# Cached keys of the paged cache fetched by one indirect transfer of GpSimd per granule, in a one-core decoder step

## The reference, cut to what matters

```python
def fox_sample(q, k_new, v_new, logf_new, pool_k, pool_v, pool_logf, page_table):
    ...
    k_all = jnp.concatenate([pool_k[page_table].reshape(b, past, h, e).astype(k_new.dtype), k_new], axis=1)
    v_all = jnp.concatenate([pool_v[page_table].reshape(b, past, h, e).astype(v_new.dtype), v_new], axis=1)
    ...
    sc = jnp.einsum('bthe,bshe->bhts', q, k_all).astype(jnp.float32) * scale + cq - ck
    ...
    p = jax.nn.softmax(sc, axis=-1)
    return jnp.einsum('bhts,bshe->bthe', p.astype(v_all.dtype), v_all).reshape(b, t, h * e)
```

## Time and profile before

| | us |
|---|---|
| median of 3 runs | 1396.51 |
| lowest, highest | 1396.45, 1398.31 |
| the profiled execution | 1398.2 |
| its span | 1396.5 |
| TensorE busy | 1320.3 (95%) |
| VectorE busy | 962.0 (69%) |
| ScalarE busy | 551.3 (39%) |
| GpSimd busy | 250.4 (18%) |
| mean granted TensorE clock | 0.976 of full speed |

### The profile page before, as it was taken

How to read it: one execution, slowest core, us unless ns; L and a number is a source line. 1 busy time by engine, 2 the same in 40 slices (tenths; PEclk the granted TensorE clock), 3 DMA queues, 4 the chain that set the end, 5 groups by cost and what they waited for, 6 DMA issues and landing times.

```text
span 1396.5 us, 24365 instructions
## 1 busy us (share of the span) xinstructions
PE 1320.3 (95%) x9293; PEld 1210.4 (87%) x9293; DVE 962.0 (69%) x1391; ACT 551.3 (39%) x908; POOL 250.4 (18%) x242
## 2 busy tenths in 40 slices
PE   6899999988986899999999999999999999999999
PEld 4668788766665767899899999999999999999999
DVE  6757789979886786758868787787888796111111
ACT  6422211145645665534544434434434454010100
POOL 5540013342331242010101101101111100000000
PEclk9799999989998999999999999999999999999999
DMA  8148766669996966432222222221222275332222
GB/s 290 57 136 255 222 189 194 195 186 250 281 268 213 332 211 193 145 102 91 77 67 86 91 76 63 90 90 55 84 92 69 69 275 188 94 93 74 86 73 73
DMA packets 153422, 201.57 MB, mean 144 GB/s; under 512 B 22005, under 2 KB 116237, under 8 KB 152897
## 3 DMA queue, kind: packets, MB, share of 16 engines
q1 hardware_dynamic: 134492, 140.12, 33.1%
q0 software_dynamic: 12848, 46.73, 11.0%
q10 hardware_dynamic: 5964, 13.16, 3.2%
HBM read 169.64 MB, written 29.82 MB: 143 GB/s over the span
## 4 chain that ended last, share of the span: by engine, by line
PE 59%; DVE 13%; SPq 8%; issue 7%; DMA 6%; POOL 3%; ACT 2%; ACTq 1%; DVEq 0%; POOLq 0%
PE ps L1274 8%; PE ps L1275 8%; PE ps L1276 8%; PE ps L1335 5%; PE ps L1336 5%; PE ps L1337 5%; SPq L411 3%; PE ps L1014 2%; SPq L410 2%; PE ps L1015 2%; PE ps L1115 2%; PE ps L1016 2%; DMA upr<-in_w_upL 2%; DMA ring<-in_cache_a_k 2%; PE ps L1138 1%
## 5 line engine op out<-in xcount | busy, mean ns | idle before, releaser
L1274 PE MATMUL ps<-hhi,uph 128*128 128x258 f32 x704 | 201.0, 285 | 4.3 <-issue 1.4
L1275 PE MATMUL ps<-hlo,uph 128*128 128x258 f32 x704 | 199.6, 284 | 0.0
L1276 PE MATMUL ps<-hhi,upl 128*128 128x258 f32 x704 | 199.3, 283 | 0.0
L1014 PE MATMUL ps<-whi,hhi 128*128 128x512 f32 (+1 forms) x376 | 146.6, 390 | 13.7 <-DVE wlo L1857 9.3
L2578 DVE TENSOR_TENSOR dnl<-dnr,dnh 128x896 fp32r<-128x896 f32 (+2 forms) x24 | 27.3, 1136 | 173.1 <-ACT dnh L1770 173.1
L1016 PE MATMUL ps<-whi,hlo 128*128 128x512 f32 (+1 forms) x376 | 143.2, 381 | 0.0
L1015 PE MATMUL ps<-wlo,hhi 128*128 128x512 f32 (+1 forms) x376 | 143.1, 381 | 0.0
L1274 PEld LDWEIGHTS ps<-hhi,uph 128*128 128x128 f32 x704 | 134.0, 190 | 6.0 <-DVE ug L2536 2.1
L1275 PEld LDWEIGHTS ps<-hlo,uph 128*128 128x128 f32 x704 | 134.2, 191 | 0.0
L1276 PEld LDWEIGHTS ps<-hhi,upl 128*128 128x128 f32 x704 | 133.9, 190 | 0.0
L2763 POOL TENSOR_TENSOR upr<-upr 128x512 f32<-128x512 f32 x22 | 29.5, 1340 | 450.4 <-DMA upr<-in_w_upL 373.8
(11 more groups left out here) (338 smaller groups left out, 3597.5 us busy)
## 6 DMA issues: line engine op xcount, KB each, us to landing
upr<-in_w_upL SPq DMA_DIRECT2D x88, 256.0 KB, 3.4
ring<-in_cache_a_k SPq DMA_DIRECT2D x168, 128.0 KB
scr_act<-va SPq DMA_DIRECT2D x22, 516.0 KB, 2.6
ring<-in_cache_a_k ACTq DMA_DIRECT2D x88, 128.0 KB
wst<-in_w_in SPq DMA_DIRECT2D x32, 256.0 KB, 4.2
fr<-scr_act SPq DMA_DIRECT2D x14, 516.0 KB, 5.5
dnr<-in_w_down SPq DMA_DIRECT2D x12, 448.0 KB, 4.4
dnr<-in_w_down SPq DMA_DIRECT2D x10, 512.0 KB, 3.8
```

Of the source, the lines that this page charges most:

```text
L1014: pe.matmul(out, lh, whi[:, sl, 0:w], start=(kc == 0), stop=False)
L1274: pe.matmul(out, hi_, r_hi[:, cs], start=(first and i == 0), stop=False, skip_group_check=not first)
L1275: pe.matmul(out, hi_, r_lo[:, cs], start=False, stop=False, skip_group_check=not first)
L1276: m = pe.matmul(out, lo_, r_hi[:, cs], start=False, stop=(i == 3), skip_group_check=not first)
```

## The change

All 64 key granules are fetched by GpSimd, each with one indirect transfer, as the values are. `load_pages` and its uses go from SP and ACT. On SP `k_load` stays for the window and memory caches alone. The new `k_page` waits for `k_used` (from granule 4 on) and issues the transfer. In the loop over the projection units it stands behind the unit's `inverse_rms`; the granules and their units are those of `K_ASK`, which is unchanged. The first four granules are requested in (0, 4) in place of (0, 5). In the loop over the value loads, `K_BEFORE` gives the key granules that are requested ahead of value load k. The wait for the row table moves to the first four granules. The window and memory caches get semaphores of their own (`cmk_ld`), and a key granule's transfer now counts 16 in place of 64.

```diff
-        kpool = t["cache_a_k"].rearrange("o n p h e -> (o n) p (h e)")
+        krows = t["cache_a_k"].rearrange("o n (p r) h e -> (o n p) (r h e)", r=4)
...
-        def load_pages(sp, pool, seq, group, slot, pages=range(4), dst=ring, sem="ring_ld"):
-
-            for j in pages:
-                page = sp.value_load(ptab[0:1, bass.ds(seq * PAGES + (group * 4 + j), 1)], min_val=0, max_val=NPOOL - 1)
-                sp.dma_start(dst[32 * j:32 * j + 32, slot, :, :].rearrange("p r c -> p (r c)"),
-                             pool[bass.ds(page, 1)].rearrange("o (p r) c -> p (o r c)", r=4))\
-                    .then_inc(S(f"{sem}{slot}"), 16)
+        def page_gather(pool, rows_, n, dst, sem):
+
+            pool.indirect_dma_start(out=dst.rearrange("p r c -> p (r c)"), out_offset=None, in_=rows_,
+                                    in_offset=bass.IndirectOffsetOnAxis(ap=gtab[:, 0, n:n + 1], axis=0)).then_inc(sem, 16)
...
+        K_BEFORE = {2: [NKP + 2], 4: [NKP + 3]}
+        for g_ in sorted(K_STEP):
+            if K_STEP[g_] + 4 < NKA:
+                K_BEFORE.setdefault(next(k_ for k_ in range(4, NV) if v_step[k_ - 4] >= g_ + 2), []).append(K_STEP[g_] + 4)
...
             def k_load(n):
 
                 sp.wait_ge(S("k_used"), n - 3)
-                if n < NKA:
-                    load_pages(sp, kpool, n // 8, n % 8, n % 4)
-                else:
-                    cm_load(sp, ring[:, n % 4], n - NKA, S(f"ring_ld{n % 4}"), "k")
+                cm_load(sp, ring[:, n % 4], n - NKA, S(f"cmk_ld{n % 4}"), "k")
...
-                if k == (0, 5):
-                    sp.wait_ge(S("const_ld"), 96)
-                    sp.wait_ge(S("x_split"), 3 * KC)
-                    sp.wait_ge(S("x_sq"), 3 * KC)
-                    for s4 in range(4):
-                        load_pages(sp, kpool, 0, s4, s4)
...
-                for n in K_ASK[u]:
-                    sp.wait_ge(S("k_used"), n - 3)
-                    load_pages(sp, kpool, n // 8, n % 8, n % 4, (0, 1))
...
-                if k in ((4, 6), (4, 7)):
-                    k_load(NKP + k[1] - 6)
...
-            k_load(NKP + 2)
...
-            k_load(NKP + 3)
             for g in range(STEPS):
                 H, s = divmod(g, NT)
-                if g - 2 in K_STEP:
+                if g - 2 in K_STEP and K_STEP[g - 2] + 4 >= NKA:
                     k_load(K_STEP[g - 2] + 4)
...
-                for n in K_ASK[u]:
-                    act.wait_ge(S("k_used"), n - 3)
-                    load_pages(act, kpool, n // 8, n % 8, n % 4, (2, 3))
...
+            def k_page(n):
+                if n >= 4:
+                    pool.wait_ge(S("k_used"), n - 3)
+                page_gather(pool, krows, n, ring[:, n % 4], S(f"ring_ld{n % 4}"))
+
...
                     inverse_rms(rsn[0:r, i % 2, 0:nh], ssn[0:r, i % 2, 0:nh], HD, "rs_norm", i + 1)
+                if k == (0, 4):
+                    pool.wait_ge(S("g_rows"), 1)
+                    pool.wait_ge(S("x_split"), 3 * KC)
+                    pool.wait_ge(S("x_sq"), 3 * KC)
+                    for n in range(4):
+                        k_page(n)
+                for n in K_ASK[u]:
+                    k_page(n)
+                if k in ((4, 6), (4, 7)):
+                    k_page(NKP + k[1] - 6)
...
-            pool.wait_ge(S("g_rows"), 1)
             for k in range(NV):
+                for n in K_BEFORE.get(k, ()):
+                    k_page(n)
```

More of the change, by code:

```diff
@@ L524, in k_total @@
         def k_total(n):
-            return 64 * (n // 4 + 1) if n < NKA else 64 * (NKA // 4) + 16 * ((n - NKA) // 4 + 1)
+            return 16 * (n // 4 + 1)
         SET_END = {}
@@ L2223, in cm_dot @@
                 T_.wait("qb_ld", 32 if grp == DIL else 48)
-                T_.wait(f"ring_ld{i % 4}", k_total(NKA + i))
+                T_.wait(f"cmk_ld{i % 4}", 16 * (i // 4 + 1))
                 link(dve.tensor_tensor(kv, kv, qb[0:nk, b0:b0 + 4, :], ALU.mult))
@@ L2727, in v_load @@
                 if k < NVA:
-                    pool.indirect_dma_start(out=vring[:, k % 4].rearrange("p r c -> p (r c)"), out_offset=None, in_=vrows,
-                                            in_offset=bass.IndirectOffsetOnAxis(ap=gtab[:, 0, k:k + 1], axis=0))\
-                        .then_inc(S(f"vr_ld{k % 4}"), 16)
+                    page_gather(pool, vrows, k, vring[:, k % 4], S(f"vr_ld{k % 4}"))
                 else:
```

## The result

The kernel with the change takes 1421.5 us (median of 4 runs, 1417.8 to 1421.9) against 1397.3 us of the kernel before (4 runs, 1396.5 to 1398.3): ratio 1.017, 95% interval 1.015 to 1.019. It is 24.2 us slower; predicted were 1418.7, 22.2 slower. The spans of the two profiled executions are 1420.1 and 1396.5. One execution of all those reported here stood apart, 6332 us in e3, and is in no ratio.

What follows compares the result with a forecast made beforehand. TensorE was taken to bound the projections, VectorE to have no slack in block 4, and DMA engines to be full in the attention. -4 + 29.4 + 0.8 - 4 = +22.2 us gave 1418.7, range 1403 to 1434.

Steps and rivals of the forecast that it cites:

- The five delays: Block 4, units (4, 1) to (4, 5): VectorE waits for gathers requested behind the inverse root, 5.9 us each, +29.4 us.
- Block 3: Granules used two units after request there; delays of 0 to 1 us in two or three places, counted 0, up to +3.
- The first four granules: Four gathers in (0, 4) hold up the next inverse root some 3 us; TensorE's lead of four units hides it: 0.
- The relief of the projections: SP and ACT lose page requests, so TensorE's waits and lower clock there shrink: -4 us, between 0 and 5.8.
- Granule 48: Requested between the last two inverse roots of the projections, taking up GpSimd's time: +0.8 us.
- The attention: Granules 50 to 63 move from SP's queue to GpSimd's; VectorE's waits for keys go: -4 us, between -14 and +15.
- No byte is saved, and the DMA engines stay full: Attention: moving key granules to GpSimd leaves bytes and DMA load unchanged; share before was 1.05 up to 430 us.
- I don't count `qb`: Attention: VectorE's 6.12 us wait for `qb` was left out, since SP, waking at 408.90 from `k_used`, wasn't late.
- (a): Rival: no VectorE wait in block 4 as gathers are out early; pure relief, about -12 us, 1384; 10 in 100.
- (b): Rival: block 4's delays come but relief is twice as large, -14 in the attention, -5.8 before: +10, 1407; 15 in 100.
- (c): Rival: gathers take longer than 4.1 us beside other traffic, or values suffer in the attention: +36, 1433; 17 in 100.
- (d): Rival: nothing moves, since bytes and DMA engines are the same and SP's and ACT's idle time was free; 3 in 100.

Runs made afterwards that it cites:

- e3: Kernel before, with only the attention's key granules 48 to 63 gathered by GpSimd; projections keep pages of SP and ACT: 1393.3 us, ratio to before 0.997.
- e1: Kernel after, with each projection unit's gathers moved ahead of its inverse root in GpSimd's queue: 1391.2 us, ratio to before 0.996; second run 1389.8, 0.996.
- e6: Kernel after, with gathers moved ahead of the inverse root in units (4, 0) and (4, 2) alone: 1408.2 us, ratio to before 1.010.
- e4: Kernel before, with SP and ACT holding back block 4's page requests until the unit's inverse root is done: 1429.6 us, ratio to before 1.025.
- e2: Kernel after, with gathers moved ahead of the inverse root in block 4 alone, block 3 unchanged: 1395.5 us, ratio to before 0.999.
- e7: As e5 up to granule 47, but the attention's granules 48 to 63 are SP's page loads as before: 1399.3 us, ratio to before 1.003.
- e5: e1 with each gather asked for one unit earlier, still ahead of the inverse root: 1391.0 us, ratio to before 0.997.
- e8: Kernel after, with each gather asked for one unit earlier, still behind the inverse root: 1390.9 us, ratio to before 0.995.
- e9: e3 with GpSimd sending the attention's keys as four direct 128 KB page transfers per granule, not one gather: 1407.6 us, ratio to before 1.007.

## Why the prediction was right

**The five delays: 29.4 predicted, 30.6 measured.** The place, the number, the engine that waits and the second granule's cover were as forecast. From issue to VectorE's start the way took 4.73, 4.04, 4.35, 4.61 and 4.93 us, mean 4.5, where the row gave 4.1. GpSimd's first root instruction, L2656, took 0.20 there and L2659 1.02 to 1.04. From the sum of (4, "S") to that of (4, 5) 66.35 us passed in place of 35.33: +31.0. e1 and e6 show that this is the loss, e4 that it is the moment and not the kind of transfer.

The Trainium skill ("DMA: Bandwidth & Descriptors", on the anatomy of a DMA of GpSimd's path) gives an estimate of 3.2 us for 512 KB by its rate and its fixed 2.0 us, which it says are setup and completion. The runs show 4.0 to 4.9 from the start of the issuing instruction, so the page's figure is 0.8 to 1.7 us short for a gather here; the 1.04 to 1.05 us for which GpSimd executes the instruction are about as much. The measured 4.5 decides.

**Block 3: counted 0, "up to +3".** Mis-sized: two waits, 4.4 us, of which some 2 us are left at (4, "S") (e2).

**The first four granules: counted 0.** As forecast: VectorE's wait for the next root is 5.21 us in place of 2.04, 0.9 us of it is left at the second sum of squares after it (106.77 against 105.88), and TensorE's waits from 80 to 130 us are 0.6 us in all, 0.5 before.

**The relief of the projections: -4 predicted.** The sum of (4, "S") came at 250.40 in place of 255.69, -5.3, the waits of block 3 included. But 3.3 us of this are in the execution of before that was profiled: e3 and e4, the same code up to there, have 252.40 and 252.39; VectorE's waits for keys up to there are 6.3 us in it and 4.1 in e3. What was left is 2.0, and with block 3's waits gone 4.8 (e1, 247.65). At the start of the attention it is worth nothing: 298.60 in e1 against 298.73 in e3. The small waits for keys of block 4, 4.8 us in e1, are as much as was left; e7 shows no gain at the end from GpSimd's keys in the projections. So the term fits the profile it was made against by luck, and was too large for the kernel.

**Granule 48: +0.8 predicted.** From the sum of (4, 5) to the first matmul 10.5 us passed in place of 11.0, so -0.5.

**The attention: -4 predicted, -4.3 measured**, from 278.4 to 274.2 us, but the size is luck: TensorE's idle time in it fell by 9.4 us (33.9 to 24.5, see e7), and its busy time rose by 5.1 at a granted clock of 0.92 in place of 0.94. The kernels with gathers whose clock there is 0.94, as before, gained 6.4 to 9.1 (e1, e3, e5, e6). "No byte is saved, and the DMA engines stay full" failed: from 340 to 400 us the share is 0.88 in e5 in place of 1.05, at a higher rate. "I don't count `qb`: SP wasn't late there" failed as well. SP woke at 408.90, but its next requests then took long to go out, 6.75 and 4.04 us ahead of the one for `qb`. Before:

```profile
409.79 6.75 SPq L599 DMA_DIRECT2D kst<-o_kc  x1
416.58 4.04 SPq L438 DMA_DIRECT2D ring<-in_cache_c_k  x1
420.72 2.05 SPq L704 DMA_DIRECT2D qb<-scr_qs  x1
```

and after the change:

```profile
431.24 0.57 SPq L600 DMA_DIRECT2D kst<-o_kc  x1
436.33 0.37 SPq L435 DMA_DIRECT2D ring<-in_cache_c_k  x1
436.80 0.45 SPq L689 DMA_DIRECT2D qb<-scr_qs  x1
```

The waits for `qb` and of TensorE behind it go from 6.12 and 9.73 to these:

```profile
DVE ring L2207 <- DMA qb<-scr_qs: 3.1, 1, 3.1
PE ps L1104 <- DVE oN L2197: 6.7, 1, 6.7
```

The other kernels with gathers in the attention have 269.3 to 274.1 us there (e1 twice, e2, e3, e5, e6, e8), of which 24.2 to 26.4 are TensorE's idle time; those with page loads have 275.0 (e4), 278.4 (before), 282.4 (e7) and 286.1 (e9), with 27.4 to 34.0 idle. The longer pause ahead of the attention may have a part in it: e4 has the pause and page loads, and its 275.0 is near the 274.2 of the kernel after. That it isn't the whole is shown by e3.

The sum of the steps is in the trace: -5.3 + 31.0 - 0.5 = +25.2 at the start of the attention, -4.3 in it, and +2.7 from there to the end (818.7 us after, 816.05 before). For that last stretch, which no kernel changes, the other kernels here have 815.9 to 819.9 us, so the 2.7 is no effect of the change that can be told.

By whole times the account is shorter. The order of the gathers alone is the step from e1's ratio to that of the kernel after, 0.996 to 1.017, 29 us for 30.6 us of waits. All the rest of the change is e1 against before, -0.004, some 5.5 us; predicted were -4 + 0.8 - 4 = -7.2. So the term that carries the forecast was right for the reason given, and the small ones came to about the right sum with luck in two of them.

**The rivals.** (a), no wait in block 4, is what e1 made of the kernel: it then was 1391, not 1384, since the projections' part of the relief comes to nothing. (b) had the attention gain 14: it gained 4.3, and 6.4 to 9.1 at the clock of before. (c) had gathers of 6.8 us or values that suffer; the gathers took 4.0 to 4.9, and TensorE's waits for values from 300 to 600 us went to under 0.5 us in all. (d) would have needed delays of 1.6 us. The rule of the Trainium skill that it names (same page, "Issuing engines are not separate DMA queues") says that transfers run on the same 16 DMA engines whichever engine starts them, and that starting them from several saves only the issuing time. e9 agrees, with 3.78 us per MB against 3.79 of the kernel before; in e3 the form of the transfer changes with the engine, which the rule doesn't speak of.

## What to carry to other kernels

When a prefetch moves into an in-order queue, look at what stands ahead of it: a request behind a wait for the consumer's own last step is no prefetch, and each loop pays root, issue and transfer in full (here 6.1 us, five times). One index or two swapped lines turned 1.7% slower into 0.4 to 0.5% faster. An idle issuing engine is worth little by itself; fewer and larger transfers and a queue that doesn't block the next request can be worth some us where the DMA engines are full.

## What the runs showed of the hardware

- **A page load costs the DMA engines more than a gather of the same bytes.** Over the whole run the queues that carried pages (q1, q10) fell from 33.1% and 3.2% of 1396.5 us to 26.2% and 0.4% of 1420.1, 129 us less for 33.6 MB; q0 rose from 11.0% to 17.4%, 93.5 us more for the same bytes. That is 3.8 against 2.8 us of 16 engines per MB, and 12288 packets against 9216:

```profile
q1 hardware_dynamic: 134492, 140.12, 33.1%
q0 software_dynamic: 12848, 46.73, 11.0%
q10 hardware_dynamic: 5964, 13.16, 3.2%
```

```profile
q1 hardware_dynamic: 126428, 118.09, 26.2%
q0 software_dynamic: 22064, 80.29, 17.4%
q10 hardware_dynamic: 1740, 1.62, 0.4%
```

- **GpSimd's times depend on what VectorE does.** The first root instruction takes 0.20 us beside an idle VectorE, 0.19 beside one of its sums (e5, at 257.36), and 1.10 beside its multiplication; a gather's issue takes 0.94 to 2.40 us, 2.02 where VectorE multiplies (e5 above).
- **The same matmuls cost TensorE by the granted clock.** In the attention 2086 or 2087 recorded matmuls are busy 244.5 us at a mean clock of 0.94, 249.6 at 0.92 and 253.2 at 0.91 (before, after, e7), a spread as large as what the changes there were worth. A stretch is best compared between executions of like clock.
- **One profiled execution can hold a delay of its own.** The kernel before reached the attention at 302.04, and the same code in e3 at 298.73; two thirds of the 3.3 us are longer waits for keys. A term of 4 us made from one execution should carry that much doubt.
